# Two queues for the expert weights: the gate matrices issued by ScalarE, the up and down matrices by the sync engine

## The reference, cut to what matters

```python
g = xblk @ w_gate[e] + b_gate[e]
u = xblk @ w_up[e] + b_up[e]
g = jnp.minimum(g, SWIGLU_LIMIT)
u = jnp.clip(u, -SWIGLU_LIMIT, SWIGLU_LIMIT)
a = (u + 1.0) * (g * jax.nn.sigmoid(SWIGLU_ALPHA * g))
return a @ w_down[e] + b_down[e]
```

## Time and profile before

| what | value |
|---|---|
| median of three runs | 1255.01 us |
| the profiled execution | 1258.08 us |
| its span, first to last instruction | 1256.2 us |
| PE matmuls busy | 1209.4 us, 96% of the span |
| DVE busy | 492.0 us, 39% |
| ACT busy | 192.1 us, 15% |
| q1, SP's queue | 448.71 MB, 86.6% of 16 engines' span |
| q10, ACT's queue | 3.47 MB, 0.8% |
| HBM read | 457.64 MB, 367 GB/s over the span |
| gate, up, down halves: issue to landing | 23.6, 26.3, 28.3 us (medians) |
| PE's clock, mean granted | 0.993 |

### The profile page before, as it was taken

How to read it: one execution, slowest core, us unless ns; L and a number is a source line. 1 busy time by engine, 2 the same in 40 slices (tenths; PEclk the granted TensorE clock), 3 DMA queues, 4 the chain that set the end, 5 groups by cost and what they waited for, 6 DMA issues and landing times.

```text
span 1256.2 us, 15360 instructions
## 1 busy us (share of the span) xinstructions
PE 1209.4 (96%) x5768; PEld 491.1 (39%) x5768; DVE 492.0 (39%) x1189; ACT 192.1 (15%) x400; POOL 8.1 (1%) x12
## 2 busy tenths in 40 slices
PE   7999999999999999999998999999999999999997
PEld 3665664555333333333333333333333333333332
DVE  2299882345433334323332323233234233343223
ACT  3204443133101110010010001100010000100102
POOL 0000010000000000000000000000000000000000
PEclk9999999999999999999999999999999999999999
DMA  9915566828799999999999999999999999999995
GB/s 339 337 62 175 150 226 252 359 90 323 306 429 426 427 426 427 425 429 427 427 427 427 427 428 427 425 429 427 426 377 385 426 426 426 425 426 428 426 424 213
DMA packets 53539, 461.29 MB, mean 367 GB/s; under 512 B 6249, under 2 KB 15913, under 8 KB 27815
## 3 DMA queue, kind: packets, MB, share of 16 engines
q1 hardware_dynamic: 51119, 448.71, 86.6%
q0 software_dynamic: 1152, 8.39, 1.8%
q10 hardware_dynamic: 1216, 3.47, 0.8%
HBM read 457.64 MB, written 3.28 MB: 367 GB/s over the span
## 4 chain that ended last, share of the span: by engine, by line
PE 79%; DMA 18%; DVE 1%; issue 1%; ACT 1%; SPq 0%; ACTq 0%; DVEq 0%
PE psum L889 42%; DMA ring<-in_w_up 14%; PE psum L869 6%; PE psum L345 5%; PE psum L935 4%; PE psum L407 3%; DMA ring<-in_w_gate 3%; PE psum L617 2%; PE psum L391 1%; PE psum L919 1%; PE psum L743 1%; DMA ring<-in_w_mk 1%; PE psum L544 1%; PE psum L750 1%; PE psum L415 1%; PE psum L588 1%
## 5 line engine op out<-in xcount | busy, mean ns | idle before, releaser
L889 PE MATMUL psum<-ring,work 128*64 128x512 f32 x3072 | 678.8, 597 | 20.7 <-DMA ring<-in_w_up 18.5
L889 PEld LDWEIGHTS psum<-ring,work 128*64 128x64 f32 x3072 | 216.6, 137 | 470.8 <-issue 417.3
L869 PE MATMUL psum<-H,work 128*64 128x512 f32 (+1 forms) x384 | 92.7, 600 | 0.0
L2249 DVE TENSOR_TENSOR work<-psum,keep 128x512 f32<-128x512 f32 x16 | 11.1, 692 | 167.2 <-PE psum L889 167.2
L1802 DVE SCALAR_TENSOR_TENSOR ring<-ring,vecT 128x256 f32<-128x256 f32 x240 | 72.6, 380 | 0.1
L2235 DVE TENSOR_TENSOR X<-X,psum 128x512 f32<-128x512 f32 x63 | 43.2, 686 | 64.6 <-PE psum L935 64.6
L2249 DVE TENSOR_TENSOR work<-psum,work 128x512 f32<-128x512 f32 x16 | 11.1, 692 | 142.2 <-PE psum L889 142.1
L1660 ACT COPY work<-psum 64x512 f32<-64x512 f32 x32 | 18.5, 579 | 297.9 <-PE psum L889 297.9
L1648 ACT COPY work<-psum 128x512 f32<-128x512 f32 x31 | 18.2, 587 | 279.1 <-PE psum L869 279.1
L1639 ACT ACTIVATE work<-work 128x512 f32<-128x512 f32 x32 | 20.2, 631 | 220.6 <-DVE work L2326 220.6
L345 PEld LDWEIGHTS psum<-C,work 128*128 128x128 f32 (+1 forms) x332 | 44.2, 191 | 24.5 <-issue 21.1
(11 more groups left out here) (338 smaller groups left out, 966.0 us busy)
## 6 DMA issues: line engine op xcount, KB each, us to landing
ring<-in_w_gate SPq DMA_DIRECT2D x64, 2048.0 KB, 23.6
ring<-in_w_up SPq DMA_DIRECT2D x63, 2048.0 KB, 26.3
ring<-in_w_down SPq DMA_DIRECT2D x63, 2048.0 KB, 28.3
ring<-in_cache_keys SPq DMA_DIRECT2D x64, 144.0 KB, 2.6
ring<-in_w_in SPq DMA_DIRECT2D x1, 4096.0 KB, 33.9
ring<-in_mem_keys_turned SPq DMA_DIRECT2D x8, 512.0 KB, 14.1
ring<-in_cache_mem_v SPq DMA_DIRECT2D x8, 512.0 KB, 6.7
ring<-in_w_in SPq DMA_DIRECT2D x1, 2688.0 KB, 24.5
```

What stands on the lines that cost most here:

```text
L869: last = mm(psum[64 * nh:64 * nh + 64, 2, :], Ph[0:ROWS[tt], tt, :], xn[0:ROWS[tt], tt, 512 * nh:512 * nh + 512], start=tt == 0, stop=tt == 2)
L889: last = mm(psum[64 * nh:64 * nh + 64, bank, :], src[:, j, 64 * half:64 * half + 64], w[:, half, j, 512 * nh:512 * nh + 512], start=first ...
L2249: v.tensor_tensor(gm, psum[:, 0, :], B[b][:, 0:512], ALU.add).then_inc(s.g_sum, 1)
```

## The change

`refill` on SP no longer issues the gate matrices in the loop. It keeps the wait for the first half of the freed slot, the wait for `u_clip` and the bias rows. A new function on ACT, `load_gate`, issues both halves of the gate matrix of turn t + 2 at the end of turn t, behind the two copies of the down product. It reads the expert's number out of `order` itself. ACT waits once for `order` ahead of its loop. The first two gate matrices, which are loaded ahead of the loop, stay with SP, and so do all up and down matrices. `weights` is moved so that both engines can call it.

```diff
--- before.py
+++ after.py
@@ -318,6 +318,11 @@
 
         def slot(m):
             return ring[:, 8192 * m:8192 * (m + 1)].rearrange("p (h j n) -> p h j n", h=2, j=4)
+
+        def weights(kind, e):
+            w = a[("w_gate", "w_up", "w_down")[kind]]
+            w = w[0, e] if isinstance(e, int) else w[0, bass.ds(e, 1)].rearrange("a k n -> (a k) n")
+            return w.rearrange("(h p j) n -> h p (j n)", h=2, j=4)
 
         def rows_of(w):
             return w.rearrange("(k p) n -> p k n", p=P)
@@ -1262,11 +1267,6 @@
             for b in range(DEC_B):
                 memory_keys(b)
 
-            def weights(kind, e):
-                w = a[("w_gate", "w_up", "w_down")[kind]]
-                w = w[0, e] if isinstance(e, int) else w[0, bass.ds(e, 1)].rearrange("a k n -> (a k) n")
-                return w.rearrange("(h p j) n -> h p (j n)", h=2, j=4)
-
             def load_bias(b, e):
 
                 row = a["bias_rows"][e] if isinstance(e, int) else a["bias_rows"][bass.ds(e, 1)].rearrange("a r n -> (a r) n")
@@ -1308,10 +1308,13 @@
                 m = 4 + l
                 src = weights(m % 3, e)
                 for half in range(2):
+                    if m % 3 == 0:
+                        if half == 0:
+                            sp.wait_ge(ring_used[m % 4][0], i * 3 + m // 4)
+                            sp.wait_ge(s.u_clip, i * 4 + m // 3)
+                            load_bias((m // 3) % 2, e)
+                        continue
                     sp.wait_ge(ring_used[m % 4][half], i * 3 + m // 4)
-                    if m % 3 == 0 and half == 0:
-                        sp.wait_ge(s.u_clip, i * 4 + m // 3)
-                        load_bias((m // 3) % 2, e)
                     if last_one and half:
                         load_end(m, src, s.end_up if m % 3 == 1 else s.end_down)
                     else:
@@ -1632,6 +1635,18 @@
             act.wait_ge(s.gt_full, 1)
             nc.scalar.copy(PgT[1][0:NE, :], psum[0:NE, 5, 0:T]).then_inc(s.pgt_moved, 1)
 
+            def load_gate(i, q):
+
+                l = (3 * q + 2) % 4
+                at = i * 4 + q + 2
+                if isinstance(at, int) and at >= NE:
+                    return
+                at = slice(at, at + 1) if isinstance(at, int) else bass.ds(at, 1)
+                e = act.value_load(order[0:1, at], min_val=0, max_val=NE - 1)
+                for half in range(2):
+                    dma(slot(l)[:, half].rearrange("p j n -> p (j n)"),
+                        weights(0, e)[half]).then_inc(ring_in[l][half], 16)
+
             def expert(i, q, twice=False, last_one=False):
 
                 e = i * 4 + q
@@ -1664,7 +1679,9 @@
                 if twice:
                     act.wait_ge(ring_used[m % 4][1], i * 3 + (m // 4 + 1))
                     nc.scalar.copy(Yx, psum[:, 5, 0:256]).then_inc(s.ov_ym, 1)
-
+                load_gate(i, q)
+
+            act.wait_ge(s.order_ready, 1)
             with act.Fori(0, TWICE // 4) as i:
                 for q in range(4):
                     expert(i, q)
```

## The result

The changed kernel takes 1277.24 us (median of 4 runs, 1275.5 to 1279.97), the kernel before 1254.5 us beside it (4 runs, 1253.49 to 1256.26). The ratio is 1.0171, with a 95% interval of 1.0153 to 1.019. It is slower by 22.7 us (19.2 to 23.8 by the interval); 21.4 were forecast. Its profiled execution took 1275.5 us, with a span of 1273.7 us against 1256.2 before.

A forecast was written before the change was run, and what follows sets the result against it. The prediction took DMA, then PE after the long turn 20, to bound the kernel. Delays of 11.4 + 10.0 = 21.4 us on the median 1255.01 gave 1276.4 us, range 1262 to 1289.

The forecast's parts named there:

- The bound: DMA sets the pace from 560 to 885 us, two turns taking 59.37 us; PE does from 960 to 1243 us.
- Part 1, the late issue: The gate half that wakes the dry DMA, at 340.97 and 967.77 us, is issued 4.35 and 4.37 us later on ACT.
- the lower bound of 3.2 us: Lateness of the first gate issue at 341 us if ACT's sequencer runs ahead of its copies.
- Part 2, overtaking: Queues alternate by packet, so gate arrives before the preceding turn's second down half, which lands 9.8 us later, less its slack.
- The slack of 2.7 us: At turn 19 the second down half landed at 878.3 us, 2.7 us before PE came to it at 881.0.
- the sum: Total delay: 11.4 us up to turn 20 plus 10.0 us from there to the end, 21.4 us.
- The signs: Expected in the profile after: faster gate landings, second down halves over 40 us, waits on down, PE 11 then 21 us late.
- Service by age: Rival, chance 0.15: packets go out roughly in order of issue, so only lateness costs, at most 8.7 us; 1264 us.
- A loss or gain of bandwidth: Two rivals: two streams cost bandwidth (chance 0.15, 1288 us at 1.5%) or give it (0.05, 1245 us at 4%).
- That it is hidden: Rival, chance 0.03: the ring's eight halves absorb the delay and the wait only changes its name; 1255 us.

The follow-up runs named there:

- e1: Kernel before, all transfers still in SP's queue, but the gate refill waits until the second down half is used and the down product copied; 1264.32 us, ratio 1.0059.
- e2: Changed kernel, but each gate half is issued on ACT's queue as soon as its half of the slot is used, ahead of the copies; 1267.11 us, ratio 1.0093.
- e3: Changed kernel, but only the second half of each gate matrix goes through ACT's queue, the first stays with SP; 1268.77 us, ratio 1.0102.
- e6: Changed kernel, with each gate half loaded as two transfers of every second 4 KB row, giving short packets; 1350.37 us, ratio 1.0739.
- e8: Kernel before, with only the 16 KB of bias rows per turn moved to ACT's queue, issued in mid-turn; 1254.56 us, ratio 0.9997.
- e5: Kernel before, with both halves of every down matrix on ACT's queue, issued behind the copy of the gathered tokens; 1277.78 us, ratio 1.0169.
- e7: As e3, but each second gate half is issued behind the sigmoid of the next turn, some 8 us later; 1262.41 us, ratio 1.006.
- e4: Changed kernel, with gate transfers written as 4 KB rows, which still went out as 16 KB packets; 1275.11 us, ratio 1.0168.

## Why the prediction was right, step by step

**The bound.** Right. Two turns in the DMA-bound stretch take 59.40 us and the rate is 427 GB/s.

**Part 1, the late issue.** Right in kind, too large in size: 3.5 and 3.2 us where 4.35 and 4.37 were forecast. The step that failed is "since the instructions stand behind each other on one engine". ACT issues its transfer 0.98 and 0.67 us behind the start of its first copy, while the copies still run, and the lower bound of 3.2 us was the right one. e1 shows what lateness costs without overtaking, 5.9 us of the loop.

**Part 2, overtaking.** Right: 9.9 us at turn 19 for 9.8 forecast. The slack of 2.7 us came off it: 13.4 - 2.7 = 10.7, and 10.8 us is what the loop lost. At turn 30: 3.2 + 9.8 - 4.2 = 8.8, and the loop lost 8.2 (10.0 forecast). With the issue's true lateness the sum is 10.6 + 8.8 = 19.4 us against 19.0 measured; the 0.4 us between them are the gate matrix at turn 30, 9.4 us for 9.8. The 21.4 us of the forecast are 2.4 more than the loop lost, 2.0 of them by the lateness, and only 1.3 less than the medians' 22.7. That they come so near the medians is in part luck. What the sum did not look at is the slack of the up halves: in the change it was never used up (no wait for up is left), in e2 and e3 it was.

**The signs.** The second down half took 39.1 us to land at turn 19 and 40.73 us at 611 us, where over 40 were forecast, and PE was 10.8 us late at turn 20 and 19.0 at the end, where 11 and 21 were. The DMA's restarts came 3.5 and 3.2 us later, not 4.4. Gate halves in 16.5 us, waits for down alone and 59.40 us for two turns came as said.

**The rivals.** Service by age falls by the landing times of the changed kernel and by e6. A loss or gain of bandwidth falls by the 427 GB/s; what is lower, 360 GB/s from 885 to 960 us where it was 406, is the DMA standing dry for longer behind the long turn, not slower transfers. That it is hidden falls by the result. "Issuing engines are not separate DMA queues", the section of the Trainium skill's page "DMA: Bandwidth & Descriptors" that speaks for no change, holds where nothing that counts is overtaken (e8, ratio 0.9997) and not where something is (1.0171). e2 and e5 are what shows the order of service as the larger cause: it stays when the lateness goes, and its waits move when another matrix overtakes.

**Not settled.** The 1.4 us between e1 + e2 and the change; the 3.7 us between the loop and the medians; the first part of e5's loss; and e7's size, of which I only have the list of waits.

## What to carry to other kernels

When one ordered stream fills the DMA engines, its single queue is also its schedule: here a second queue added no bandwidth (427 GB/s with one and with two), and let the part that it carried overtake transfers that were needed sooner. Before moving a transfer, list all halves that it will pass with the slack of each, since the smallest slack sets the price, and look where the DMA runs dry, because there a late issue was a loss for good (e1). If two queues have to share, look at the packet sizes: they set the shares in e6.

## What the runs showed of the hardware

**Short spells at half clock behind a wait or a pause.** PE's clock in the changed kernel, windows in the columns of the earlier trace rows, around a wait for down that ends at 533 us, and around the one at 652.5 us:

```profile
530.00:533.00 3.00, 0.59 (x4) 0.00 (x0) 0.46 (x3) 0.00 (x0) 0.00 (x0) 1.00 1.02 426
533.50:537.00 3.50, 3.31 (x8) 1.01 (x10) 1.31 (x2) 0.00 (x0) 0.00 (x0) 0.51 1.02 435
653.00:656.50 3.50, 3.50 (x12) 1.05 (x10) 1.03 (x1) 0.00 (x0) 0.00 (x0) 0.51 1.02 435
```

PE stood for most of 530 to 533 us (0.59 us busy), and behind it the granted clock is 0.51, the lower of the two levels (1.2 GHz), for about 3.4 us. The kernel before, with waits of at most 1.3 us, has no such spell between 338 and 885 us. I had not expected a price for how the waiting is cut into pieces. Where PE waits for the DMA anyway it is nothing: two turns across the spell at 653 us still take 711.91 - 652.50 = 59.41 us by the chain, and e4 has one spell more, at 1141 us, with 0.3 us less in the loop.

Where PE sets the pace it has a price. In turn 21 PE pauses for 1.53 us just ahead of 960 us, in the kernel before and in e8 alike. The window behind it, in the kernel before and in e8:

```profile
960.00:965.00 5.00, 4.77 (x18) 1.57 (x20) 3.40 (x11) 0.00 (x0) 0.00 (x0) 0.67 1.03 439
```

```profile
960.00:965.00 5.00, 4.94 (x28) 1.61 (x26) 3.76 (x10) 0.00 (x0) 0.00 (x0) 1.00 0.99 410
```

At 0.67 PE runs 2 x 0.33 x 5 = 3.3 us at half speed, which costs 1.7 us, and turn 21 is 1.7 us longer in the kernel before than in e8. The changed kernel, e1, e2, e3 and e4 have the spell too; e5 and e7 have not. So the same pause is followed by a spell in one execution and not in another, and a loop time that is compared over one execution each can be off by 1.7 us.

**The same spells ahead of the loop, and the spread between executions.** The windows of 120 to 180 us in e3 and in e7, where the two kernels have the same work:

```profile
120.00:180.00 60.00, 58.53 (x500) 39.08 (x500) 53.51 (x162) 27.18 (x77) 4.83 (x5) 0.94 0.53 170
```

```profile
120.00:180.00 60.00, 57.81 (x526) 39.60 (x526) 56.05 (x167) 28.23 (x78) 4.82 (x5) 1.00 0.56 175
```

At 0.94 the engine runs 2 x 0.06 x 60 = 7.2 us of the 60 at half speed. e7's profiled execution had no spell up to the loop and reached the end of turn 0 at 338.9 us; e3's had several and reached it at 346.6 us. Such a difference lies ahead of anything that was changed, and it is larger than the difference of the two loops. The runs without a profile fit: of the 18 of the kernel before beside e5 to e8, the fastest took 1251.37 us at a mean clock of 0.998 and the slowest 1261.38 us at 0.990. Half speed costs 0.002 x 1249.5 = 2.5 us of the one span and 0.010 x 1259.5 = 12.6 us of the other; that is 10.1 us of difference, and 10.0 were measured. Where in these runs the spells lay is not on record.
